# Places of the on-chip buffers: every buffer at a multiple of 64 bytes, the operands of a split product alike modulo 512

## What is computed

```python
def first_block(x, mix_norm_g, w_in, ...):
    pos = jnp.arange(x.shape[1], dtype=jnp.int32)
    for l in range(DEPTH):                      # DEPTH = 2
        h = rmsnorm(x, mix_norm_g[l])
        x = x + token_mixers(h, pos, w_in[l], ...)
        h = rmsnorm(x, ffn_norm_g[l])
        if l % 2 == 0:
            x = x + swiglu(h, ffn_w1[l // 2], ffn_w3[l // 2], ffn_w2[l // 2])
        else:
            x = x + moe_ffn(h, router_w[l // 2], moe_w1[l // 2], moe_w3[l // 2], moe_w2[l // 2])
    return rmsnorm(x, final_norm_g)

def swiglu(h, w1, w3, w2):
    return (jax.nn.silu(h @ w1) * (h @ w3)) @ w2   # 1024 -> 2816 -> 1024
```

## The kernel before

| buffer | place before, bytes | modulo 512 | place after | modulo 512 |
|---|---|---|---|---|
| ring, x, low_rows, hT, hT_hi, w_hi, w_lo, merged, gates, u_z, xs, scratch, cst | 0 to 130048 | 0 | the same | 0 |
| gain, ygain, soft | 144480, 148576, 152672 | 96 | 144512, 148608, 152704 | 128 |
| small | 153760 | 160 | 153792 | 192 |
| perch, alpha_w, bc | 154400 to 155936 | 288 | 154432 to 155968 | 320 |
| gT, table | 157152, 158176 | 480 | 157184, 158208 | 0 |
| u_ret, u_gla | 158240, 166432 | 32 | 158272, 166464 | 64 |
| u_ml | 170560 | 64 | 170624 | 128 |
| ch_in, conv, probs, xdt, y, yT | 174752 to 208544 | 160 | 174848 to 208640 | 256 |
| third_gu, down_w | 158240, 174624 | 32 | 158272, 174656 | 64 |
| fhT_hi, fhT_lo, xg_lo | 199200, 201248, 203296 | 32 | 199680, 201728, 203776 | 0 |

## Time and profile before

### The profile page before, as it was taken

The page is one execution under the profiler, slowest core; times in us unless marked ns, Lnnn a source line. Parts: engine busy times, 40 slices in busy tenths (PEclk is TensorE's granted clock), DMA queues, the critical chain, the costliest instruction groups (busy, mean ns, idle before and its releaser), DMA issues.

```text
span 2692.7 us, 30881 instructions
## 1 busy us (share of the span) xinstructions
PE 2500.5 (93%) x11365; PEld 1986.7 (74%) x11365; DVE 1636.8 (61%) x2327; ACT 1320.3 (49%) x1687; POOL 407.1 (15%) x224
## 2 busy tenths in 40 slices
PE   6999899989998799999999999989998997998998
PEld 5876588878865687777777877868767885776786
DVE  1465655534565598898888988963446544244554
ACT  1343244413332387777777877834534442543443
POOL 2254100003551000000000000024520002551000
PEclk9999899999998899999999999999999998999999
DMA  6433275424241599999999999953456533346550
GB/s 196 142 110 138 99 248 185 139 91 163 94 167 64 173 368 318 322 348 307 322 349 306 331 340 315 343 156 116 151 190 224 188 119 111 135 169 217 188 188 32
DMA packets 373374, 549.30 MB, mean 204 GB/s; under 512 B 20948, under 2 KB 273224, under 8 KB 373144
## 3 DMA queue, kind: packets, MB, share of 16 engines
q1 hardware_dynamic: 369072, 535.82, 58.4%
q0 software_dynamic: 3776, 9.80, 1.3%
q10 hardware_dynamic: 432, 2.37, 0.2%
HBM read 546.91 MB, written 1.05 MB: 203 GB/s over the span
## 4 chain that ended last, share of the span: by engine, by line
PE 65%; DVE 7%; issue 2%; ACT 2%; DMA 2%; POOL 1%; DVEq 0%; SPq 0%; ACTq 0%
PE mb L863 12%; PE mb L865 12%; PE mb L864 12%; PE pb L863 5%; PE pb L865 5%; PE pb L864 5%; PE pb L841 3%; PE pb L1236 2%; PE pb L846 2%; DMA ring<-in_w_in 1%; DVE w_lo L2360 1%; POOL w_lo L719 1%; PE mb L1191 1%; PE pb L932 1%; DVE gates L1911 1%
## 5 line engine op out<-in xcount | busy, mean ns | idle before, releaser
L2360 DVE TENSOR_TENSOR w_lo<-ring,w_hi 128x1024 fp32r<-128x1024 f32 x384 | 461.6, 1223 | 177.8 <-ACT w_hi L1520 128.1
L863 PE MATMUL mb<-w_hi,hT_hi 128*128 128x512 f32 x1232 | 499.0, 405 | 10.6 <-DVE w_lo L2360 6.4
L865 PE MATMUL mb<-w_lo,hT_hi 128*128 128x512 f32 x1232 | 485.1, 394 | 0.0
L719 POOL TENSOR_TENSOR w_lo<-ring,w_hi 128x1024 fp32r<-128x1024 f32 x152 | 370.9, 2464 | 533.3 <-ACT w_hi L1520 533.0
L1520 ACT ACTIVATE w_hi<-ring 128x1024 fp32r<-128x1024 f32 x280 | 285.9, 1054 | 312.2 <-DMA ring<-in_w_in 186.8
L2360 DVE TENSOR_TENSOR w_lo<-down_w,w_hi 128x1024 fp32r<-128x1024 f32 x242 | 295.4, 1223 | 93.3 <-ACT w_hi L1520 79.1
L863 PE MATMUL pb<-w_hi,hT_hi 128*128 128x512 f32 x736 | 300.2, 408 | 10.3 <-DVE low_rows L2360 7.6
L865 PE MATMUL pb<-w_lo,hT_hi 128*128 128x512 f32 x736 | 291.7, 396 | 0.0
L864 PE MATMUL pb<-w_hi,low_rows 128*128 128x512 f32 x736 | 290.9, 395 | 0.0
L1653 ACT ACTIVATE w_hi<-ring 128x1024 fp32r<-128x1024 f32 x256 | 268.1, 1056 | 24.3 <-PE mb L865 18.6
L863 PEld LDWEIGHTS mb<-w_hi,hT_hi 128*128 128x128 f32 x1232 | 232.6, 189 | 62.2 <-DVE w_lo L2360 12.1
(11 more groups left out here) (441 smaller groups left out, 3774.9 us busy)
## 6 DMA issues: line engine op xcount, KB each, us to landing
ring<-in_moe_w SPq DMA_DIRECT2D x128, 1024.0 KB, 7.9
ring<-in_w_in SPq DMA_DIRECT2D x48, 2048.0 KB, 7.9
down_w<-in_moe_w SPq DMA_DIRECT2D x88, 1024.0 KB, 10.6
third_gu<-in_moe_w SPq DMA_DIRECT2D x48, 1024.0 KB, 8.9
down_w<-in_w_ffn_down SPq DMA_DIRECT2D x22, 1024.0 KB, 9.9
ring<-in_w_out SPq DMA_DIRECT2D x8, 2048.0 KB, 8.0
ring<-in_ffn_w SPq DMA_DIRECT2D x16, 1024.0 KB, 8.1
ring<-in_w_ffn_gate SPq DMA_DIRECT2D x16, 1024.0 KB, 5.4
```

Of the source, the lines that this page charges most:

```text
L719: nc.gpsimd.tensor_tensor(w_lo[:, m % NPIECE], source[m][0], w_hi[:, m % NPIECE].bitcast(F32), ALU.subtract).then_inc(pool_split, 1)
L863: mm(o, a_hi, hi, start=start, stop=False)
L865: return mm(o, a_hi, lo, start=False, stop=stop)
L2360: return tt(dst, src, hi.bitcast(F32), ALU.subtract)
```

## The change

A helper `in_lines` makes every buffer, and adds one of 32 bytes behind each whose size, rounded up to 32 bytes, is not a multiple of 64. Those are cst, bc, u_gla and u_ml (`ea`, the fifth, goes away: it becomes columns 150 to 157 of `small`). A buffer `down_rest` of 448 bytes behind down_w moves the three buffers after it. Nothing else is changed: the instructions, their order, the waits and the loads are the same. The table above has the places that come of it.

```diff
+STEP, LINE = 8, 16
...
+        def in_lines(stack, name, shape, dt):
+
+            tensor = stack.enter_context(nc.sbuf_tensor(name, shape, dt))
+            if -(-math.prod(shape[1:]) // STEP) * STEP % LINE:
+                stack.enter_context(nc.sbuf_tensor(name + "_rest", [P, STEP], F32))
+            return tensor
+
         def sb(name, shape, dt=F32):
-            return ctx.enter_context(nc.sbuf_tensor(name, shape, dt))
+            return in_lines(ctx, name, shape, dt)
...
-        ea = sb("ea", [P, 2, 4])
+        ea = small[:, 150:158].rearrange("p (l h) -> p l h", l=2)
...
             def mix(name, shape, dt=F32):
-                return mixers_memory.enter_context(nc.sbuf_tensor(name, shape, dt))
+                return in_lines(mixers_memory, name, shape, dt)
...
         down_w = sb("down_w", [P, NSLOT, DN_W])
+        sb("down_rest", [P, 112])
         fhT_hi = sb("fhT_hi", [P, 2, S], F32R)
...
-                    f(ea[:], bc[:, :, 4:8], ACT.Exp).then_inc(ea_ready, 1)
+                    f(ea, bc[:, :, 4:8], ACT.Exp).then_inc(ea_ready, 1)
```

More of the change, by code:

```diff
@@ L10 @@
+import math
 import numpy as np
```

## The result

The changed kernel takes 2669.12 us (median of 5 runs, 2664.95 to 2672.39), the kernel before 2686.59 us (5 runs, 2684.01 to 2691.84). The ratio is 0.9928, 95% interval 0.9910 to 0.9945: 17.5 us faster by the medians, 19.3 by the ratio, whose interval goes from 14.8 to 24.2. The forecast was 2665.5 us, the range 2656 to 2680. One run of the kernel before, at a granted clock of 0.555, took 4256.98 us; the ratios leave it out, while the median 2689.96 of the first four experiments has it in (2689.1 without it). The profiled execution has a span of 2668.5 us and took 2670.3; before it was 2692.7 and 2694.5.

The account below looks back on a forecast made before the run. TensorE was taken to bound the kernel, with the DMA right behind in the experts' stage. Gains of 16.7 - 1 + 4.9 = 20.6 us from the median 2686.1 gave 2665.5 us, range 2656 to 2680.

Parts of the forecast that it names:

- What bounds it: Whole kernel: TensorE, busy 93% of the span, bounds it; only faster issue or a shorter rare wait can pay.
- Two rhythms from the places: Feed-forward stage: products take 226.8 ns with stationary operands whole 512 bytes from the weights, 233.0 ns 32 bytes past.
- One operand in three spoils all three: Experts' gate and up products: xg_lo off slows all three distances, mean 232.6 ns, not about 228.9.
- The experts' step: Experts' stage: a step takes 8.41 us against 8.60, 0.19 us less, 16.7 us over 88 steps.
- The dense step: Three feed-forward stages: aligned down products save 0.149 us a step, 4.9 us over 33 steps.
- The DMA: Experts' stage: loads need 8.6 us a step, but 4.4 us of lead hides it; 1 us taken off.
- Everything else: Aligning down_w and third_gu gains 0 to 7 ns a copy, taken as 0; small mixer steps minus 2 to plus 1 us.
- The sum: Whole kernel: 16.7 - 1 + 4.9 = 20.6 us, from the median 2686.1 to 2665.5 us, 0.8% faster.
- Not the offset: fhT_hi, fhT_lo, xg_lo: distance or row position high up sets the rhythm; nothing changes, 2686.1 us; chance 0.13.
- Half of it: Experts' gate and up products are slow from memory load; only down products gain, 7.2 and 4.9 us, 2674.0 us; chance 0.10.
- DMA takes over: Experts' stage: lead is smaller than read, step stays 8.6 us; only 4.9 us remain, 2681.2 us; chance 0.03.
- Slower: Experts' stage reads start alike and could meet; 3960 products each lose 6.2 ns, 24.6 us, 2710.7 us; chance 0.06.

Follow-up runs that it names:

- the first four experiments: The first four follow-ups: 448 bytes removed; 480 bytes added; the same with xg_lo 32 bytes off; everything shifted 32 bytes. Kernel before: 2689.96 us.
- the move alone: Kernel before with 480 bytes ahead of fhT_hi, moving fhT_hi, fhT_lo and xg_lo, and nothing else: 2671.16 us, ratio 0.9943.
- all but the move: Changed kernel without the 448 bytes ahead of fhT_hi, so fhT_hi, fhT_lo and xg_lo lie 64 bytes off: 2686.86 us against 2689.96, ratio 0.9994.
- the shifted weights: Changed kernel with 32 bytes ahead of w_hi, moving all behind it but not hT_hi and low_rows: 2699.96 us against 2689.96, ratio 1.0043.
- the xg_lo run: Kernel before with fhT_hi and fhT_lo moved by 480 bytes, xg_lo left 32 bytes off: 2678.93 us, ratio 0.9975.

## Why the prediction was right

*What bounds it.* Right. TensorE's rhythm was the only thing that could pay, and it paid: 811.3 us between the first and last turns instead of 826.9, with the same work and nearly the same waits (one of 2.4 us for the DMA went, ahead of the first turns).

*Two rhythms from the places.* Right, and this is shown, not argued: the move alone gives all of it (811.2 us), shifting everything by 32 bytes costs nothing, and shifting the weights turns fast and slow products over.

*One operand in three spoils all three.* Right for the stationary operand: xg_lo alone gives 699.4 ns, fhT_lo alone 698.4, fhT_hi and fhT_lo together hardly more, 699.6. It was carried too far where I expected the same of w_lo (693.5 to 695.2), and the size depends on the distance: xg_lo 64 or 128 bytes off costs 10 to 12 ns a triple, 32 bytes off 17. "All three" holds for the sum alone: with xg_lo off the distances are 238, 229 and 232 to 233 ns, not three times 233.

*The experts' step.* Forecast 8.41 us, measured 8.417 (six settling distances, not five). The sum over 88 steps was 16.7, less 1 for the DMA; the stage gained 15.6 to 15.8. The size fits by luck, since the reason for the 1 is wrong: no wait for the DMA came, and the lead of the first pass held at 1.1 us and more. What is missing lies at the turn of passes: eight passes shortened by 1.97 us each, where 11 steps of 0.19 would give 2.09, because a pass's ends are not full steps.

*The dense step.* Forecast 0.149 us a step; 16.95 became 16.80. 33 steps, 4.9 us. The settling at 231.7 ns stayed, as the step's working had it.

*The DMA.* Right, and closely. I had put the DMA at 8.6 us for a step's three loads. In the trace after, the loads of a step land 8.58 us behind those of the step before (mean over the last six steps of the passes), while they are issued, and wanted by ACT, every 8.42 and 8.41 us; hence the 0.17 us of lead lost a step, close to the 0.2 that I took. So in the later steps of a pass the DMA already goes at its own pace, and only the lead hides it. The DMA share in the stage rose from 0.96 to 0.98. This is what a further gain would meet: with another 0.2 us off each step, nine steps would take 1.8 us more, which the 3.0 us left in the later passes would bear and the 1.2 us left in the first would not (an estimate; no such kernel was run).

*Everything else.* Right at 0: 1063 and 1223 ns as before, and a kernel in which these changes are undone (the move alone) has the same steps. One reason given was weak: that plain float32 products show no price was read from records of 592 ns, and the length of a record would not have shown it. The starts bear it out: 429 ns apart, in the median, for the products with ch_in and for those with merged and gates, in the kernels before and after and with the weights shifted.

*The sum.* 20.6 us forecast; the steps of the trace make 15.8 + 4.9 = 20.7; the medians show 17.5 (14.8 to 24.2). Four kernels have the fast steps: they came out 17.5, 18.8, 18.6 and 20.4 us below their own runs of before, on average 18.8; by the ratios 19.3, 15.3, 15.3 and 19.9, on average 17.5. The two profiled executions lie 24.2 us apart: 15.6 between the turns of the experts' stage, 4.6 between those of the dense stages, and 4.0 in the rest. This rest, 1338.7 us before and 1334.7 after, lies anywhere between 1329.2 and 1338.7 us in the ten traces in which hT_hi and low_rows are alike with both weights, and it is shortest in one without the gain (all but the move). So the 4.0 us, and with them the 2 or 3 between the steps and the medians, are no larger than the spread from one execution to the next; a small loss elsewhere can't be excluded. The granted clock goes along with it only in part: of the runs of before in the first four experiments those at 0.974 to 0.975 take 2682 to 2686 us and those at 0.971 to 0.972 2687 to 2695, but in the later rounds runs at 0.974 to 0.975 take 2689 to 2693.

*The rivals.* "Not the offset" fell with the shifted weights, and height with it. "Half of it" fell with the xg_lo run: the experts' gate and up products gain as soon as xg_lo is aligned, DMA share or not. "DMA takes over" fell by the waits. "Slower" fell at once; a kernel slower than before does exist, but by the same rule, not against it.

*What spoke against it.* The distance in which xg_lo is loaded 32 bytes off takes 238 ns, against 227 where it is alike with the weights. The Trainium skill ("TensorE: Matmul & The Clock Gate", section "Step-by-step: what each phase is for") has two read ports so that loading takes nothing from the stream. For these products the trace agrees only where both operands lie alike. The lines of 16 bytes in the Trainium skill ("SBUF — State Buffer", section "Specifications (TRN2)") do not give the rule either: 32, 64 and 128 bytes are whole lines and slow, 256 is fast.

## What to carry to other kernels

Where split products (fp32r) run back to back, each with its own load of the stationary operand, put stationary and moving operand a whole number of 256 bytes apart in each partition (0 and 256 modulo 512 are what was tried). Here that is 2.4% of each such matmul, 233 against 227 ns, for some hundred bytes of padding. Look for it in the distances between starts in a stretch without waits, comparing products of one form; the records of single matmuls hide it. And check every member of such a group, since one that is off took most of a triple's gain here.

## What the runs showed of the hardware that was not expected

- The rhythm of a 128x512 fp32r matmul with its own 128x128 load is 227 ns where the operands lie 0 or 256 bytes apart (modulo 512), and up to 233 ns on average where they lie 32, 64 or 128 bytes off. Tried were 0, 32, 64, 128, 256 for fhT and xg_lo, 32 bytes the other way for hT_hi and low_rows, and 32 for w_lo; no other distance was. 128 bytes rests on one execution.
- The penalty is not additive. By 32 bytes, one stationary operand off costs about 17 ns a triple, all of them off about 18, w_lo alone 11 to 14. Why, and by what part of the chip, no run here shows.
- Plain float32 matmuls of 128x512 don't have it: 429 ns from start to start (median) with ch_in 160 bytes off from ring, and 429 ns in the changed kernel, where it lies 256 bytes off, and in the run with shifted weights, 288 bytes off.
- The three loads of 1 MB of a step land 8.58 us apart as a set where the DMA is the one that lags, in the last six steps of the passes after.
- The first six distances behind a turn are 231.7 ns also where all operands are aligned, before and after. What they pay for wasn't tried.
